# Idle products, an early normalisation and an early copy of the values in a four-layer diffusion backbone

## The chip, the cores and the metric

The kernel runs on 1 core of one Trainium2 chip, in float32. The metric is the device time of one execution in microseconds, lower is better. TensorE (PE in the profile) multiplies matrices, VectorE is DVE, ScalarE is ACT, GpSimd is POOL, and SyncE (SP) issues most transfers.

## The reference

A backbone over 256 noisy latent tokens and 256 context tokens of width 1024, four layers deep. Layer `i` normalises and modulates its input, applies a token mixer of kind `i % 3`, adds the result through a gate, and then applies a gated feed-forward with a width-3 convolution:

```python
for i in range(DEPTH):                       # 4 layers; mixers A, B, C, A
    m_lat = jnp.split((s_lat @ mod_w[i] + mod_b[i])[:, None, :], N_MOD, axis=-1)
    m_ctx = jnp.split(s_ctx @ mod_w[i] + mod_b[i], N_MOD, axis=-1)
    u_lat = _modulate(_rmsnorm(h_lat, g[0]), m_lat[0], m_lat[1])
    ...
    h_lat = h_lat + m_lat[2] * _rmsnorm(o_lat, g[1])
    f_lat = _conv_ffn(_modulate(_rmsnorm(h_lat, g[2]), m_lat[3], m_lat[4]), *ffn)
    h_lat = h_lat + m_lat[5] * _rmsnorm(f_lat, g[3])
```

Mixer A (layers 0 and 3) is full attention with 8 heads of 128, with RMSNorm and rotary embedding on queries and keys. Mixer B (layer 1) is a Hyena long convolution. Mixer C (layer 2) is windowed attention with 16 heads of 64 and a sink logit per head. The softmax of C is `softmax([s0, s_ctx, s_loc])` with the sink's column left out afterwards. The context stream passes through the same layers except for the last.

## The kernel before

Each engine runs its own instruction list, written by hand, and waits on semaphores. Nothing is planned at run time. A weight tile of 1 MB is loaded by SP, split by ACT (`w_hi`) and DVE (`w_lo`) into two rounded parts, and multiplied by TensorE in three products.

**The start.** Layer 0's modulation vectors come from `mod_w[0]`, which is loaded in 24 "units" of 1 MB and 256 columns. `unit_rows(r)` (L616 to L626) multiplies unit `r` with both conditioning vectors: sixteen products into one row block. ACT copies the row (`unit_row`, L1303 to L1308), and `unit_cols` (L628 to L638) turns it into columns with four tiny products. `start_turns(p, v)` (L859 to L873) multiplies the hidden state with a diagonal matrix of inverse norms, which normalises and transposes it. Once the columns of units 0 and 1 are there, DVE makes the first coefficients (`start_mod`), ACT and DVE make the first modulated inputs, and `start_part(0, 0)` (L875 to L890) can begin with the layer's own products. Between these steps stand calls of `idle_products(n)` (L841 to L844). Each makes `n` products of 128x128 whose result nobody reads, and each product has two records in the trace. There are four calls in `before`: 8, 12, 4 and 6 products.

**Layer 0's attention.** Heads and token blocks make pieces `x`. For each, TensorE makes the scores, DVE finds their maximum (`peak`, `negate`), ACT makes exponentials (`exps`), DVE divides by the sum (`normalise`), TensorE transposes (`turn`), ACT copies, and TensorE multiplies with the values (`pv`). On DVE `step(x)` is `normalise(x)` followed by `peak(x + 2)` and `negate(x + 2)`. Before, DVE does `step(-2)`, `step(-1)`, then `finish_mod(0, 1)` and only then `step(0)`. `finish_mod(0, 1)` (L1645 to L1671) waits for the columns of all 24 units and finishes layer 0's gates. On TensorE the last unit's columns stand right after the value tile (`unit_cols()` at L1180), and `turn_gates(0)` stands ahead of the scores of piece 3 (L975). ACT makes the exponentials of piece 1 after it has copied the row of unit 23.

**Layer 2's attention.** Here two heads go together (STEP is 2). Tile 5 of the input projection gives the values. Before, TensorE makes the scores of pieces 0 to 3 after tile 5, then `turn_v` (L953 to L959) transposes the values. ACT does `exps(2, 0)`, `exps(2, 1)`, then `evac(5)`, which copies the value tile out with its bias (L1407), and then the copy of the transposed values (L1428). `turn_v` waits for `evac(5)`.

Of the kernel before, what the change touches and what calls it, by code (L numbers as in the profile page):

```python
# [40 lines left out]
KIND = [i % 3 for i in range(DEPTH)]  # L41
# [129 lines left out]
def build(nc, a, out):  # L171

    es = ExitStack()
    with es:
# [167 lines left out]
        STEP = {i: 1 if KIND[i] == 0 else 2 for i in ATT}  # L342
# [152 lines left out]
        k = MOD0  # L495
# [87 lines left out]
        def _(pe):  # L583
# [44 lines left out]
            def unit_cols():  # L628

                if not turning:  # L630
                    return
                r = turning.pop()
                pe.wait_ge(group_rows, r + 1)
                for cc in range(2):
                    c = 2 * UNIT_COLS[r] + cc
                    last = mm(modp[:, c:c + NMOD * KT + 1:NMOD * KT], MROW[:, r % 2, cc * P:(cc + 1) * P], pick,
                              start=True, stop=True)
                last.then_inc(group_cols, 1)  # L638
# [202 lines left out]
            def idle_products(n):  # L841

                for _ in range(n):
                    mm(bank[3][:, 0:P], ident, PR[:, 0, :], start=True, stop=True)  # L844

            pe.wait_ge(rows_in, 16 * N_ROW_DMAS[0])
            turn_rows(range(EARLY))
            idle_products(8)
            pe.wait_ge(consts_set, 1)
            pe.wait_ge(par_ready, 1)  # L850
            pe.wait_ge(silu_ready, 1)
# [1 line left out]
            def start_unit(r):  # L853

                if r % 2 == 0 and r > 0:
                    pe.wait_ge(mod_final, r // 2)
                unit_rows(r)
# [31 lines left out]
                    last.then_inc(tile_done, 1)  # L889

            start_turns(0, 0)
            idle_products(12)
            start_unit(0)
            unit_cols()
            start_turns(0, 1)
            start_unit(1)
            unit_cols()
            idle_products(4)
            start_unit(2)
            idle_products(6)  # L900
            start_part(0, 0)
            unit_cols()
            pe.wait_ge(rows_late, 16 * N_ROW_DMAS[1])
# [57 lines left out]
            def scores(i, xs):  # L961

                A, G, part = KIND[i] == 0, ahead(NH, i), HEADS[i] // 2
                subs = 1 if HALVES[i][xs[0]][1] < 2 else 2
                for x in xs:
                    h, t = HALVES[i][x]
                    pe.wait_ge(q_roped, roped(i, h))
                    if x >= 4:
                        pe.wait_ge(s_exp, G + x - 3)
                    elif x < 2:  # L970
                        pe.wait_ge(q_roped, turns_ahead(i) + 9 + x)
                    elif x == 2 and A:
                        pe.wait_ge(q_root, norms_ahead(i) + 3)
                    elif x == 3 and i == 0:
                        turn_gates(0)  # L975
                        pe.wait_ge(gr_rows, 1)
                for b in range(subs):
                    for x in xs:
                        h, t = HALVES[i][x]
                        if A:  # L980
                            q, k = QK[:, h, :], QK[:, 8 + h // part, :]
                        else:
                            ps = slice(64 * (h % 2), 64 * (h % 2) + 64)
                            q, k = QK[ps, h // 2, :], KD[ps, h // part, :]
                        if t < 2:
                            ins = mm(s_bank(x), q[:, t * P:(t + 1) * P], k, start=True, stop=True)
                        else:
                            ins = mm(s_bank(x)[:, b * CTX:(b + 1) * CTX], q[:, SEQ + b * P:SEQ + (b + 1) * P],
                                     k[:, SEQ:TOK], start=True, stop=True)
                        if b == subs - 1:  # L990
                            ins.then_inc(s_ready, 1)
# [153 lines left out]
            for i in range(DEPTH):  # L1145
                N = NL[i]
                n0, q0 = FIRST["in", i], PAIR0["in", i]
                if KIND[i] == 1:
                    first_tiles(n0, q0, 2 * i, (TOK, TOK))
                    filter_stage(1)  # L1150
                    for t in range(2, 12):
                        tile(n0 + t, q0 + t, TOK, UH, UL, True, True,
                             after=(lambda k: turn_x1v(2) if k == 5 else None) if t == 11 else None)
                        filter_stage(t)
                        if t in (7, 9):
                            turn_x1v((t - 7) // 2)
                        if t in (8, 10):
                            forward(t // 2 - 4, 0)
                            forward(t // 2 - 4, 1)
                    long_conv()  # L1160
                    arrive = lambda k: pe.wait_ge(c_lo, 8 * (k // 4 + 1))
                    free = lambda b: ((c_fly, 16),)
                else:
                    if i > 0:
                        first_tiles(n0, q0, 2 * i, (N, TOK))
                    issued = 0 if KIND[i] == 2 else 3 if i == 0 else 4

                    def after(k, i=i, t=0, issued=issued):
                        for j in TURN_AT[i].get(t, {}).get(k, []):
                            turn_q(i, j)  # L1170
                        if t == 5 and k == 6:
                            for x in range(issued):
                                scores(i, [x])

                    for t in range(2, 6 if KIND[i] else 5):
                        tile(n0 + t, q0 + t, TOK if t == 5 else N, UH, UL, True, True,
                             after=lambda k, t=t, after=after: after(k, t=t))
                    if KIND[i] == 0:
                        value_tile(n0 + 5, q0 + 5, lambda k, after=after: after(k, t=5))
                    unit_cols()  # L1180
                    while issued < 4 and i > 0:
                        scores(i, range(issued, issued + STEP[i]))
                        issued += STEP[i]
                    for j in range(VCH[i]):
                        turn_v(i, j)
                    attention(i, issued)
                    arrive = lambda k, G=ahead(GROUPS, i): pe.wait_ge(ao_lo, G + k + 1)
                    free = lambda b, i=i: ((p_evac, ahead(NH, i) + NH[i]),) if b < 2 else ((ao_lo, ahead(GROUPS, i) + GROUPS[i] - 3 + b),)

                x_phase(2 * i, UH, UL, arrive, free)  # L1190

                n0, q0 = FIRST["up", i], PAIR0["up", i]
                first_tiles(n0, q0, 2 * i + 1, (N, N))
                for t in range(2, FM):
                    tile(n0 + t, q0 + t, N, UH, UL, True, True)
                x_phase(2 * i + 1, MH, ML, lambda k, b=i * FM: pe.wait_ge(ml_ready, b + k + 1),
                        lambda b, q=q0 + FM: (released(q - 2 + b // 2),))
# [3 lines left out]
        def _(act):  # L1201
# [175 lines left out]
            def attention_in(i):  # L1377
                n0, q0, A = FIRST["in", i], PAIR0["in", i], KIND[i] == 0
# [30 lines left out]
                for t in range(6):  # L1409
                    for k in range(KT):  # L1410
                        for j in TURN_AT[i].get(t, {}).get(k, []):
                            if A and TURNS[i][j] >= 7:
                                q_norm(TURNS[i][j])
                        if n0 + t in UNITS and k % 2 == 1:
                            unit_row(UNITS[n0 + t][k // 2])
                        if t == 5 and k == 5:
                            exps(i, 0)
                    if KIND[i] == 2 and t == 3:
                        bias_hi(i)
                    if t < 5:  # L1420
                        hi(n0 + t + 2)
                    else:
                        exps(i, 1)
                    act.wait_ge(tile_done, n0 + t + 1)
                    evac(t)
                for j in range(VCH[i]):
                    act.wait_ge(v_turned, ahead(VCH, i) + j + 1)
                    f(VT[:, :, j * P:(j + 1) * P], o_bank(i, j).rearrange("p (k d) -> p k d", k=4),  # L1428
                      ACT.Copy).then_inc(v_ready, 1)
# [140 lines left out]
        def _(dve):  # L1570
# [254 lines left out]
            def attention(i):  # L1825
# [62 lines left out]
                    link(ts(q3[0], q3[0], scale, None, ALU.mult))  # L1888
                step(-2)
                step(-1)  # L1890
                if i == 0:
                    finish_mod(0, 1)
                for s in range(NH[i] // W):
                    if s >= KN + 3 and (s - KN - 3) % KN == 0:
                        o_lo((s - KN - 3) // KN)
                    for x in range(W * s, W * s + W):
                        step(x)
                    if s in (4, 5):
                        lo_half(FIRST["out", i] + 1, s - 4)
                for g in range((NH[i] // W - 1 - KN - 3) // KN + 1, GROUPS[i]):  # L1900
# [333 lines left out]
```

## Time and profile before

| | |
|---|---|
| Median of 3 runs | 2180.26 us (2178.58 to 2181.62) |
| The profiled execution | 2182.26 us, of which the span is 2180.5 us |
| Granted TensorE clock, mean over the span | 0.997 |
| PE busy | 2128.0 us, 98% |
| DVE busy | 1448.6 us, 66% |
| ACT busy | 885.2 us, 41% |
| POOL busy | 189.9 us, 9% |

The busy time of an engine is the union of its instructions' spans. The chain that ended last is followed back from the last instruction: at each step to whatever released it. Its shares are PE 86%, DVE 6%, ACT 4%, DMA 2% and issue 1%.

### The profile page before, as it was taken

The numbers are of one execution on the slowest core, as the hardware profiler recorded it, in microseconds if no ns is written. First come the engines' busy times: TensorE is split into PE (matmuls) and PEld (weight loads), VectorE is DVE, ScalarE is ACT, GpSimd is POOL, SyncE is SP. The second block draws the span as 40 slices with busy tenths as digits, with TensorE's granted clock in tenths as the row PEclk, the third lists the DMA queues.
The fourth block names the chain that finished last, engine by engine and source line by source line (L and its number), as shares of the span: only waits on it lengthen the run. The fifth ranks groups of instructions, "written<-read, shape, count | busy, mean of one in ns | idle before, by whom it ended". The sixth has DMA issues, their size and how long they took to land.

```text
span 2180.5 us, 28793 instructions
## 1 busy us (share of the span) xinstructions
PE 2128.0 (98%) x11716; PEld 1749.8 (80%) x11716; DVE 1448.6 (66%) x2200; ACT 885.2 (41%) x1344; POOL 189.9 (9%) x234
## 2 busy tenths in 40 slices
PE   7999999999999999999999998999999999999998
PEld 6777888888787778988888796588888878968996
DVE  3426658878767685578787656855788775656554
ACT  3336443332244433533331245844333223455543
POOL 1000011111010002011110001101111100100110
PEclk9999999999999999999999999999999999999999
DMA  9650335546542212245546531022555553314554
GB/s 317 197 186 12 116 107 164 174 154 206 201 142 96 88 58 78 78 145 164 169 152 220 174 108 59 21 93 91 163 159 169 196 193 122 98 57 147 176 191 145
DMA packets 224404, 304.44 MB, mean 140 GB/s; under 512 B 6860, under 2 KB 152906, under 8 KB 224145
## 3 DMA queue, kind: packets, MB, share of 16 engines
q1 hardware_dynamic: 219904, 289.84, 41.0%
q0 software_dynamic: 3984, 12.60, 1.9%
q8 instruction: 93, 1.52, 0.3%
q14 instruction: 39, 0.31, 0.0%
q10 hardware_dynamic: 384, 0.17, 0.0%
HBM read 301.47 MB, written 1.11 MB: 139 GB/s over the span
## 4 chain that ended last, share of the span: by engine, by line
PE 86%; DVE 6%; ACT 4%; DMA 2%; issue 1%; ACTq 0%; POOL 0%; DVEq 0%
PE lo L658 16%; PE lo L659 16%; PE lo L660 16%; PE lo L758 5%; PE lo L760 5%; PE lo L759 5%; PE hi L758 2%; PE hi L760 2%; PE hi L759 2%; PE lo L1010 2%; ACT w_hi L1210 1%; DMA w_raw<-in_ffn_w_down 1%; DVE w_lo L1586 1%; PE stat L758 1%; PE stat L759 1%
## 5 line engine op out<-in xcount | busy, mean ns | idle before, releaser
L658 PE MATMUL lo<-u_hi,w_hi 128*128 128x512 f32 (+1 forms) x1984 | 703.5, 355 | 3.1 <-DVE conv L2058 1.3
L659 PE MATMUL lo<-u_lo,w_hi 128*128 128x512 f32 (+1 forms) x1984 | 692.2, 349 | 0.0
L660 PE MATMUL lo<-u_hi,w_lo 128*128 128x512 f32 (+1 forms) x1984 | 691.9, 349 | 0.0
L1586 DVE TENSOR_TENSOR w_lo<-w_raw,w_hi 128x2048 fp32r<-128x2048 f32 (+1 forms) x179 | 399.7, 2233 | 336.3 <-ACT w_hi L1210 334.9
L1210 ACT ACTIVATE w_hi<-w_raw 128x2048 fp32r<-128x2048 f32 (+1 forms) x179 | 334.1, 1867 | 487.1 <-DMA w_raw<-in_ffn_w_down 260.9
L658 PEld LDWEIGHTS lo<-u_hi,w_hi 128*128 128x128 f32 x1984 | 376.2, 190 | 63.2 <-issue 14.5
L660 PEld LDWEIGHTS lo<-u_hi,w_lo 128*128 128x128 f32 x1984 | 376.1, 190 | 48.1
L659 PEld LDWEIGHTS lo<-u_lo,w_hi 128*128 128x128 f32 x1984 | 376.2, 190 | 47.2 <-issue 1.0
L1612 DVE SCALAR_TENSOR_TENSOR mod_acc<-mod_raw,silu_c,mod_acc 128x512 f32<-128x512 f32 x504 | 394.4, 848 | 8.9 <-DMA mod_raw<-in_mod_w 8.9
L2167 POOL TENSOR_TENSOR mid_lo<-conv,mid_hi 128x512 fp32r<-128x512 f32 (+1 forms) x88 | 117.5, 1355 | 1051.5 <-ACT mid_hi L1565 1051.5
L758 PE MATMUL lo<-w_hi,mid_hi 128*128 128x512 f32 x374 | 147.6, 395 | 3.2 <-DVE u_raw L1686 2.4
L759 PE MATMUL lo<-w_lo,mid_hi 128*128 128x512 f32 x374 | 145.9, 390 | 0.0
L760 PE MATMUL lo<-w_hi,mid_lo 128*128 128x512 f32 x374 | 145.8, 390 | 0.0
L1554 ACT ACTIVATE conv<-lo,par 128x512 f32<-128x512 f32 (+1 forms) x88 | 58.8, 719 | 145.6 <-PE lo L660 145.6
L1565 ACT ACTIVATE mid_hi<-conv 128x512 fp32r<-128x512 f32 (+1 forms) x88 | 46.6, 577 | 154.3 <-DVE conv L2058 154.3
L2044 DVE SCALAR_TENSOR_TENSOR conv<-lo,par,conv 128x510 f32<-128x510 f32 (+1 forms) x88 | 56.3, 680 | 60.5 <-ACT conv L1554 60.5
L758 PEld LDWEIGHTS lo<-w_hi,mid_hi 128*128 128x128 f32 x374 | 70.2, 188 | 21.2 <-issue 5.4
L760 PEld LDWEIGHTS lo<-w_hi,mid_lo 128*128 128x128 f32 x374 | 70.2, 188 | 15.0
L759 PEld LDWEIGHTS lo<-w_lo,mid_hi 128*128 128x128 f32 x374 | 70.3, 188 | 14.0
L1559 ACT ACTIVATE conv<-conv 128x512 f32<-128x512 f32 (+1 forms) x88 | 50.7, 579 | 71.5 <-DVE conv L2049 70.7
L1010 PEld LDWEIGHTS lo<-ident,probs 128*128 128x128 f32 x352 | 39.3, 143 | 34.0 <-DVE probs L1864 23.0
L1010 PE MATMUL lo<-ident,probs 128*128 128x128 f32 x352 | 56.1, 286 | 10.3 <-DVE probs L1864 9.9
(403 smaller groups left out, 2803.6 us busy)
## 6 DMA issues: line engine op xcount, KB each, us to landing
w_raw<-in_ffn_w_up SPq DMA_DIRECT2D x88, 1024.0 KB, 5.1
mod_raw<-in_mod_w SPq DMA_DIRECT2D x144, 512.0 KB, 4.0
w_raw<-in_ffn_w_down SPq DMA_DIRECT2D x40, 1024.0 KB, 5.1
mod_unit<-in_mod_w SPq DMA_DIRECT2D x24, 1024.0 KB, 6.6
w_raw<-in_a_w_qkv SPq DMA_DIRECT2D x12, 1024.0 KB, 7.2
w_raw<-in_b_w_in SPq DMA_DIRECT2D x12, 1024.0 KB, 5.2
w_raw<-in_a_w_out SPq DMA_DIRECT2D x8, 1024.0 KB, 5.0
w_raw<-in_ffn_w_down SPq DMA_DIRECT2D x8, 512.0 KB, 3.7
```

The costliest lines, as they stand in the source:

```text
L658: mm(o, h3[:, k, c], x, start=(first and k == 0), stop=False)
L659: mm(o, h3[:, k, c], y, start=False, stop=False)
L660: ins = mm(o, l3[:, k, c], x, start=False, stop=(last and k == nr - 1))
L758: mm(o, X[:, kt + j, s], h3[:, j, :], start=first, stop=False)
L759: mm(o, X[:, kt + j, s], l3[:, j, :], start=False, stop=False)
L760: return mm(o, Y[:, kt + j, s], h3[:, j, :], start=False, stop=last)
L1010: last = nc.tensor.transpose(t_bank(i, x)[:, at * P:(at + 1) * P], p[:, src:src + P], ident)
L1210: f(WH[:, n % 3, 0:words], RAW[:, n % 3, 0:words], ACT.Copy).then_inc(hi_ready, 1)
L1554: f(CV[:, m, 0:N], bank[2 * ((q0 + 2 * s) % 2) + m][:, 0:N], ACT.Identity, scale=col("ffn_conv_w", (3 * i + 1) * FM + c), bias=col("ffn_co ...
L1586: tt(WL[:, n % 3, 0:words], RAW[:, n % 3, 0:words], WH[:, n % 3, 0:words].bitcast(F32), ALU.subtract).then_inc(lo_ready, 1)
L1612: stt(acc, MR[:, k % 2, j, :], S2[:, s:s + 1], acc, ALU.mult, ALU.add).then_inc(mod_step, 1)
L2167: tt(ML[:, c, 0:N], CV[:, c % 2, 0:N], MH[:, c, 0:N].bitcast(F32), ALU.subtract).then_inc(ml_ready, 1)
```

## The change

There are three edits.

1. At the start the first call of idle products grows from 8 to 12, the call of 12 ahead of unit 0 goes, and the two calls of 4 and 6 around unit 2 become one of 4 behind it.
2. In layer 0 DVE does `step(0)` ahead of `finish_mod(0, 1)`. TensorE's `unit_cols()` for unit 23 moves behind the first `turn`, into the scores of piece 3 just ahead of `turn_gates(0)`. ACT makes the exponentials of piece 1 ahead of the row of unit 23.
3. In layer 2 the scores of pieces 0 and 1 move into tile 5, behind its step k = 6. ACT copies the value tile and the transposed values ahead of the exponentials of pieces 0 and 1.

```diff
             turn_rows(range(EARLY))
-            idle_products(8)
+            idle_products(12)
...
             start_turns(0, 0)
-            idle_products(12)
             start_unit(0)
             unit_cols()
             start_turns(0, 1)
             start_unit(1)
             unit_cols()
+            start_unit(2)
             idle_products(4)
-            start_unit(2)
-            idle_products(6)
             start_part(0, 0)
...
                     elif x == 3 and i == 0:
+                        unit_cols()
                         turn_gates(0)
...
-                    issued = 0 if KIND[i] == 2 else 3 if i == 0 else 4
+                    issued = 2 if KIND[i] == 2 else 3 if i == 0 else 4
...
                         if t == 5 and k == 6:
-                            for x in range(issued):
-                                scores(i, [x])
+                            for x in range(0, issued, STEP[i]):
+                                scores(i, range(x, x + STEP[i]))
...
-                    unit_cols()
                     while issued < 4 and i > 0:
...
-                        if t == 5 and k == 5:
+                        if t == 5 and k == 5 and A:
                             exps(i, 0)
+                            exps(i, 1)
                     if KIND[i] == 2 and t == 3:
                         bias_hi(i)
                     if t < 5:
                         hi(n0 + t + 2)
-                    else:
-                        exps(i, 1)
                     act.wait_ge(tile_done, n0 + t + 1)
                     evac(t)
+                if not A:
+                    exps(i, 0)
+                    exps(i, 1)
                 for j in range(VCH[i]):
...
                 step(-1)
-                if i == 0:
-                    finish_mod(0, 1)
                 for s in range(NH[i] // W):
...
                     for x in range(W * s, W * s + W):
                         step(x)
+                    if s + i == 0:
+                        finish_mod(0, 1)
```

## Rows read from the trace of the kernel before

**Rows 1.** The page's busy times: engine, us, share, instructions.
```profile
PE 2128.0 (98%) x11716; PEld 1749.8 (80%) x11716; DVE 1448.6 (66%) x2200; ACT 885.2 (41%) x1344; POOL 189.9 (9%) x234
```

**Rows 2.** PE's waits over the span: total us, times, longest us.
```profile
PE lo L1010 <- DVE probs L1864: 9.9, 13, 1.7
...
PE lo L745 <- DVE conv L1706: 2.9, 2, 2.6
...
PE lo L958 <- ACT qkv L1407: 2.1, 1, 2.1
```

**Rows 3.** PE's timeline at the start: start us, us, line, operation, [idle before].
```profile
13.61 2.05 PE L871 MATMUL stat<-conv,h 128*128 128x128 f32 x8 [2.20 <-DVE conv L1706]
15.45 4.61 PE L844 MATMUL lo<-par_rows,ident 128*128 128x128 f32 x24
19.99 1.07 PE L624 MATMUL modp<-mod_unit,silu_c 128*32 128x256 f32 x16
21.56 0.61 PE L636 MATMUL modp<-ident,mod_rows 128*128 128x2 f32 x4 [0.50 <-ACT mod_rows L1308]
22.03 1.14 PE L871 MATMUL hi<-conv,h 128*128 128x128 f32 x8
...
29.58 0.47 PE L885 MATMUL lo<-u_hi,w_hi 128*128 128x512 f32 x1 [0.77 <-DVE u_lo L1643]
```

**Rows 4.** SP's timeline: the issue of unit 0.
```profile
4.63 2.33 SPq L547 DMA_DIRECT2D mod_unit<-in_mod_w  x1
```

**Rows 5.** The DMA view of that transfer: KB, us from issue to landing.
```profile
mod_unit<-in_mod_w SPq DMA_DIRECT2D x1, 1024.0 KB, 12.6
```

**Rows 6.** Idle products, early and late: ns min/median/max, first and last start.
```profile
L844 PE MATMUL lo<-par_rows,ident x16: 420/421/422, 7.8 to 11.0; 128*128 128x128 f32 x16
...
L844 PE MATMUL lo<-par_rows,ident x7: 274/275/312, 19.1 to 19.8; 128*128 128x128 f32 x7
```

**Rows 7.** Two stretches: busy us by engine; the number after POOL is the granted clock.
```profile
155.50:162.00 6.50, 5.07 (x10) 2.42 (x11) 3.82 (x15) 2.99 (x9) 1.66 (x3) 0.51 0.22 83
1978.30:1981.30 3.00, 2.52 (x14) 2.25 (x13) 2.29 (x7) 3.00 (x8) 0.00 (x0) 0.52 0.00 1
```

**Rows 8.** PE's timeline in layer 0's attention.
```profile
156.57 1.11 PE L1010 MATMUL lo<-ident,probs 128*128 128x128 f32 x4 [1.69 <-DVE probs L1864]
...
158.26 2.08 PE L986 MATMUL modp<-qkv 128*128 128x512 f32 x2 [0.36 <-ACT gate_rows L1265]
```

**Rows 9.** ACT's timeline there: the exponentials of piece 0.
```profile
150.31 0.78 ACT L1365 ACTIVATE probs<-hi,small,q_scale 128x512 f32<-128x512 f32 x1 [1.76 <-DVE small L1852]
```

**Rows 10.** DVE's timeline there: the first of `finish_mod`, and `normalise(0)` behind it.
```profile
154.92 0.29 DVE L1659 TENSOR_TENSOR modv<-modp,par 128x32 f32<-128x32 f32 x2 [3.86 <-PE modp L636]
...
156.03 0.49 DVE L1864 TENSOR_SCALAR probs<-probs,small 128x512 f32<-128x512 f32 x1
```

**Rows 11.** PE's timeline in layer 2, from the scores of pieces 0 and 1.
```profile
1333.52 1.13 PE L986 MATMUL hi<-k_dup,qkv 64*128 64x512 f32 x4
...
1337.62 0.66 PE L958 MATMUL lo<-ident,qkv 128*128 128x128 f32 x4 [2.11 <-ACT qkv L1407]
```

**Rows 12.** ACT's timeline in layer 2.
```profile
1331.88 1.28 ACT L1365 ACT_TABLE_LOAD   x1 [3.34 <-POOL probs L2106]
1335.48 0.72 ACT L1365 ACTIVATE probs<-probs,small 128x513 f32<-128x513 f32 x1 [2.32 <-DVE small L1842]
...
1336.90 0.66 ACT L1407 ACTIVATE qkv<-lo,par 128x512 f32<-128x512 f32 x1
1338.31 0.60 ACT L1428 ACTIVATE v_tok<-lo 128x512 f32<-128x512 f32 x1 [0.75 <-PE lo L958]
```

**Rows 13.** DVE's timeline in layer 2: the scaling that ends `normalise(0)`.
```profile
1336.52 0.49 DVE L1864 TENSOR_SCALAR probs<-probs,small 128x512 f32<-128x512 f32 x1
```

**Rows 14.** ACT's timeline at another table load, with no wait behind it.
```profile
572.72 1.28 ACT L1274 ACT_TABLE_LOAD   x1
574.02 0.20 ACT L1274 ACTIVATE inv_o<-eps 128x1 f32<-128x1 f32 x1
```

## The prediction, made before the result was known

> **What bounds the kernel now.** I read the page's busy times first: PE is busy 98% of the span, no other engine over 66% [rows 1]. So the change can only win by taking out PE's idle time, or time in which PE runs slowly. The second view is PE's waits [rows 2]. The reader is to see there that the largest wait is for `normalise` (9.9 us in 13 waits, longest 1.7), and that the wait for layer 2's value copy is one wait of 2.1 us. The third view is the timeline around the three places that the diff touches, and the fourth the lengths and the granted clock there.
>
> These lengths show something that the mean clock of 0.997 hides. The idle products last 421 ns early in the kernel and 275 ns from 19.1 us on [rows 6]. The first is the length at 1.2 GHz, the second at 2.4. The granted clock is 0.51 from 155.5 to 162, in layer 0's attention, and 0.52 at 1978 [rows 7]. Before the first of these PE had waited 0.5 us and then 1.69 us, with only small products between [rows 8]. Before the second it had waited 2.6 us [rows 2]. After the 2.11 us wait of layer 2 the four products of `turn_v` take 0.66 us [rows 11], which is the length at the high clock. So of PE's waits near two microseconds some went with a fall of the clock and one did not.
>
> **Edit 1, the start.** The first call's four more products, at 0.42 us each (two records of 0.21 us spacing), take 1.7 us of the 2.20 us in which PE waits for the first diagonals [rows 3], so they cost nothing. The 12 products after `start_turns(0, 0)` run from 15.45 until the rows of unit 0 at 19.99 [rows 3]. Unit 0 landed at 4.63 + 12.6 = 17.2 us [rows 4, 5]. So its rows can begin at 17.25, which is 2.7 us earlier and no more, since the transfer ends the wait next. With all at the high clock, everything up to `start_part(0, 0)` moves by 2.7 us: the chain from the columns through the coefficients to its first product at 29.58 [rows 3] has no other long wait.
>
> But the clock rose at 19.1, in the midst of those 12 products [rows 6]. Without them PE is idle from about 15.5 to 17.2, after having been idle for the rest of the first gap. I expect the low clock in the following chain. At the low clock `start_turns` takes 2.05 us, not 1.14 [rows 3]: 0.9 more. The rows of a unit (1.07 us, [rows 3]) I double: 0.9 more for each of two. The columns (0.61 us) take some 0.35 more, twice. That is 0.9 + 1.8 + 0.7 = 3.4, and 3.4 - 2.7 = +0.7 us. I take +0.7. The ends: -2.7 if the clock stays high. On the other side the twelve products of `start_part(0, 0)` may still run at the low clock, because four idle products ahead of them cover less than ten did. They stand 0.23 us apart at the high clock and would stand 0.43 apart: 2.4 more, so +3.1. Of what was moved, `start_unit(2)` issues nothing to SP, but the transfers of units 8 to 10 wait for its group and its neighbours. They are not needed for another 20 us.
>
> The Trainium skill's page "TensorE: Matmul & The Clock Gate", section "Part 1: The HAM clock gate (the "warmup" mystery)", says that the half rate is the default and that activity releases it. By that rule idle products are not idle, which speaks against this edit. The trace agrees: 421 ns, then 275 ns, with nothing but such products in between [rows 6]. By the rule the term is +0.7, by the issue order alone it would be -2.7.
>
> **Edit 2, layer 0.** Piece 0's exponentials are finished at 151.2 [rows 9], but DVE's `normalise(0)` stands behind `finish_mod`, which starts at 154.92, so its scaling comes at 156.03 [rows 10] and PE waits 1.69 us [rows 8]. Afterwards `normalise(0)` and `peak(2)` run at 151.2, beside the value tile. The first `turn` (0.5 us at the high clock) goes into the half microsecond in which PE waits for ACT's copy of unit 23's row (the [0.50] of such a copy in rows 3). The columns then end at 154.88 as before (156.57 - 1.69). What is late next is the gates: `finish_mod` still takes until 155.8 [rows 10], and the gates' transposition with ACT's copy takes some 0.7 us. So the scores of piece 3 start at 156.5 in place of 158.26 [rows 8]: 1.7 us earlier. ACT's exponentials of piece 1, moved ahead of the row of unit 23, run at 151.2 to 152.2 where ACT had nothing, and delay no one.
>
> The rest is clock. From 156.57 to 162 all is at half speed [rows 7]: in 158.26 to 161.8 four records of scores take 3.6 us that take 1.8 at the high clock. With the `turn` in the earlier wait, PE's rest is 1.0 and 0.4 us in place of 1.69 and 0.36. If the clock stays up the term is 1.7 + 1.7 = -3.4 (the ACT and DVE steps behind it allow about that). If it falls all the same, -1.7. The rows speak equally for both, so I take the middle, -2.6. The ends are -3.4 and -1.3, the latter if the low stretch lies worse.
>
> **Edit 3, layer 2.** Scores of pieces 0 and 1 take 0.96 us wherever they stand, and the last scores end at 1335.5 (1337.62 - 2.11) as before [rows 11]. Their inputs are there by 1332.2, so the place inside tile 5 does not stall. DVE's first peak then comes 0.7 us earlier. But `exps` now stands behind both copies. The value tile is copied at 1334.75 to 1335.4, hidden by the scores. `turn_v` follows at 1335.5, and the copy of the values at 1336.2 takes 0.60 [rows 12]: 1336.8. Before, ACT's table load (1.28 us) stood right ahead of the first exponentials and ran at 1331.88, while ACT was waiting anyway [rows 12]. It now comes behind the copy: 1336.8 to 1338.1. Where no wait follows such a load, the next activation starts 1.30 us after its start [rows 14]. So the first exponentials start at 1338.1 in place of 1335.48. From there to the end of `normalise(0)` is 1.5 us (1335.48 to 1336.52 + 0.49, [rows 12, 13]). The first `turn` starts at 1339.65, where before it stood behind `turn_v` at 1338.1: 1.5 us late. Piece 1 loses more. DVE does `peak(2)` (0.7 us) between the two normalisations, and before this fitted into the wait for `turn_v`. The second `turn` comes at 1340.95 and the scores of pieces 4 and 5 at 1341.4 in place of 1339.1. In the next pair part of that is caught up, and 2.1 us stay, since this stretch is bound by DVE and ACT and not by PE.
>
> PE's wait grows from 2.11 to 3.55 us (1336.1 to 1339.65). This is longer than the 2.6 us that cost the clock at 1978 [rows 2, 7], so I expect the low clock. It costs up to 2.9 us, the half of layer 0's stretch of 5.7 [rows 7, 8], but here PE has waits of its own that take up a part. I take +1.5, so +3.6 for the edit. The ends are +0.8 (the load hidden after all, and no fall) and +5.0.
>
> The Trainium skill's "ScalarE: Activation LUTs", section "What ACT_TABLE_LOAD costs", gives about 1.28 us for the load and as much again and a little more for a drain, 2.66 in all. The trace agrees with the load and shows no drain (1.30 in all, [rows 14]). By the page's figure the term would be 1.4 us larger, an estimate.
>
> **Sum.** +0.7 - 2.6 + 3.6 = +1.7 us. The profiled execution took 2182.26 (span 2180.5 and 1.8 around it), so 2184.0 by its own time. It lies 2.0 above the median of the runs, so the forecast is 2182.0.
>
> **Rivals.**
> (a) The clock holds at the start and in layer 0, and only layer 2 loses its 2.1: -2.7 - 3.4 + 2.1 = -4.0, 2176.3. For it: 2.1 us of waiting did not lower the clock in layer 2 [rows 11]. Against: PE starts this kernel at the low clock [rows 6].
> (b) The change does what it says in all three places, with the table load hidden: -2.7 - 3.4 + 0.8 = -5.3, 2175.0. Against it is that every load stands right before its user.
> (c) Slower: the clock. PE is starved at the start and in layer 2, the low clock lasts into `start_part(0, 0)` and into the attention's first pairs: +3.1 - 1.3 + 5.0 = +6.8, 2187.1. It decides if the clock is still low when `start_part(0, 0)` begins near 30 us, and falls again near 1338. For it: [rows 7]. Against: PE recovered within 6.5 us in layer 0.
> (d) The waits are hidden by later ones anyway and nothing changes: 2180.3. Against it is that PE has hardly any idle time that could take them up.
>
> **Chances.** Forecast 0.50, (a) 0.17, (b) 0.10, (c) 0.18, (d) 0.05. No change can be told from within 0.2%, about 4.4 us. Faster than 2175.9 are most of (b) and half of (a): 0.15. Slower than 2184.6 are (c) and a tenth of the forecast's own spread: 0.22. The rest is 0.63. The range is 2176.0 to 2186.5.
>
> **What would show each step.** Rows of unit 0 at 17.25 and 1.9 us long, not 1.07; the first product of `start_part(0, 0)` at 30, not at 26.9. In layer 0 a `turn` before the columns of unit 23, and the scores of piece 3 at 1.7 us less than the shift of the start. In layer 2 a table load between the copy of the values and the first exponentials, and a wait of PE of over 3 us ahead of the first `turn`. The prediction is wrong if the start gains 2.7, if the load is not there, or if the clock stays at 1.00 in both attentions.

## The result, and the profile after

| | before | after |
|---|---|---|
| Median, 7 runs each on one chip | 2181.62 us (2178.58 to 2183.85) | 2187.82 us (2185.05 to 2189.93) |
| Span of the profiled execution | 2180.5 us | 2187.1 us |
| Granted clock, mean | 0.997 | 0.994 |

The change makes the kernel slower: the ratio of the times is 1.0032, with a 95% interval of 1.0023 to 1.0042, so 6 to 7 us (5 to 9 by the interval). The forecast was 2182.0, its range ended at 2186.5, and "slower" had a chance of 0.22. The prediction was wrong.

The page's busy times hardly move, as in [rows 1]. Only the count tells something: 28 products and 28 weight loads fewer.

```profile
PE 2128.7 (97%) x11688; PEld 1745.7 (80%) x11688; DVE 1449.4 (66%) x2200; ACT 885.5 (40%) x1344; POOL 191.0 (9%) x234
```

**The start.** PE's timeline of after, as [rows 3]: start, length, line, operation, [idle before].

```profile
8.31 4.15 PE L844 MATMUL lo<-par_rows,ident 128*128 128x128 f32 x24
14.13 1.13 PE L871 MATMUL stat<-conv,h 128*128 128x128 f32 x8 [1.67 <-DVE conv L1706]
17.74 1.86 PE L624 MATMUL modp<-mod_unit,silu_c 128*32 128x256 f32 x16 [2.48 <-DMA mod_unit<-in_mod_w]
20.96 2.05 PE L871 MATMUL hi<-conv,h 128*128 128x128 f32 x8
30.28 0.47 PE L885 MATMUL lo<-u_hi,w_hi 128*128 128x512 f32 x1 [1.56 <-DVE u_lo L1643]
...
45.92 0.63 PE L887 MATMUL lo<-u_hi,w_lo 128*128 128x512 f32 x1
46.35 0.63 PE L885 MATMUL lo<-u_hi,w_hi 128*128 128x512 f32 x1
```

The rows of unit 0 start 2.25 us earlier and take 1.86 us in place of 1.07. The first product of `start_part(0, 0)` comes 0.70 us later. Then, at 45 us, the products stand 0.43 us apart, which is the low clock. Before, they stood 0.23 apart there.

**Stretches and their clock.** The view of stretches of after (length, busy time of PE, PEld, DVE, ACT, POOL, granted clock, DMA share, GB/s), as [rows 7]:

```profile
17.90:24.60 6.70, 6.22 (x44) 3.67 (x36) 2.29 (x1) 0.49 (x2) 0.00 (x0) 0.50 1.10 348
24.70:45.10 20.40, 16.14 (x141) 11.86 (x137) 9.11 (x26) 7.36 (x14) 0.00 (x0) 1.00 1.10 350
45.20:48.50 3.30, 3.30 (x9) 2.52 (x10) 0.40 (x5) 0.00 (x0) 0.00 (x0) 0.50 1.11 350
155.50:162.00 6.50, 5.17 (x34) 3.12 (x27) 3.39 (x16) 4.24 (x12) 1.18 (x3) 1.00 0.50 164
1338.90:1352.40 13.50, 11.85 (x38) 6.07 (x40) 7.71 (x29) 9.12 (x23) 1.55 (x6) 0.50 0.01 3
```

Two low stretches are new at the start, that of layer 0 is gone, and layer 2 has one of 13.5 us.

**Layer 0.** PE's timeline of after around the gates, as [rows 8]:

```profile
156.02 0.66 PE L1009 MATMUL lo<-ident,probs 128*128 128x128 f32 x4
156.68 0.58 PE L636 MATMUL modp<-ident,mod_rows 128*128 128x2 f32 x4
158.22 0.28 PE L611 MATMUL modp<-ident,gate 128*32 128x128 f32 x1 [0.97 <-DVE gate L1669]
158.86 1.13 PE L985 MATMUL modp<-qkv 128*128 128x512 f32 x2 [0.35 <-ACT gate_rows L1263]
```

**Layer 2.** First PE's, then ACT's timeline of after, as [rows 11] and [rows 12]:

```profile
1335.59 0.66 PE L956 MATMUL lo<-ident,qkv 128*128 128x128 f32 x4
1338.23 0.66 PE L1009 MATMUL lo<-ident,probs 128*128 128x128 f32 x4 [1.98 <-DVE probs L1864]
1339.49 1.11 PE L1009 MATMUL lo<-ident,probs 128*128 128x128 f32 x4 [0.61 <-DVE probs L1864]
1340.54 2.08 PE L987 MATMUL hi<-k_dup,qkv 64*128 64x256 f32 x8
```

```profile
1334.64 0.69 ACT L1405 ACTIVATE qkv<-lo,par 128x512 f32<-128x512 f32 x1 [6.36 <-PE lo L660]
1335.35 1.28 ACT L1363 ACT_TABLE_LOAD   x1
1336.64 0.72 ACT L1363 ACTIVATE probs<-probs,small 128x513 f32<-128x513 f32 x1
1337.36 0.71 ACT L1363 ACTIVATE probs<-probs,small 128x513 f32<-128x513 f32 x1
1338.07 0.57 ACT L1428 ACTIVATE v_tok<-lo 128x512 f32<-128x512 f32 x1
```

The value tile's copy comes first, then the table load, then both exponentials, and the copy of the transposed values last. `turn_v` has no wait now, and the wait stands one step later, ahead of `turn(0)`.

**The end.** PE's last wait of after for split weights, and beside it the DMA view of the stretch in which that weight tile comes (2161.7 to 2168.5: GB/s in 40 slices, PE's instruction queue, and the transfer with its KB and its time from issue to landing):

```profile
2172.73 0.50 PE L758 MATMUL stat<-w_hi,mid_hi 128*128 128x512 f32 x1 [2.82 <-DVE w_lo L1586]
```

```profile
GB/s 0 96 0 0 0 0 72 133 12 60 24 157 313 386 398 386 386 386 373 446 398 386 398 361 398 362 109 12 12 24 24 24 24 24 24 24 36 0 0 0
...
q8 instruction: 1, 0.02, 1.0%
w_raw<-in_ffn_w_down SPq DMA_DIRECT2D x1, 1024.0 KB, 6.6
```

Before, the tile of the same number landed in 5.0 us and PE waited 1.22. Nothing of the change stands in this part of the code. The difference of the traces, point by point, counted at the issues of weight tiles, is this (after less before, us):

| | first product | 66 us | 235 us | 1315 us | 1465 us | last tile, 2157 us | end |
|---|---|---|---|---|---|---|---|
| after | +0.70 | +2.30 | -0.73 | -0.26 | +5.39 | +5.03 | +6.65 |

So the start loses (1.6 between the first product and 66 us), layer 0 gains 3.0, layer 2 loses 5.65, and the last tile's wait loses 1.6 more. One trace can't say what of this is the change and what is chance. In the seven kernels of this document that keep the start of before (two of them with a filler in PE's first wait), the first product comes anywhere from 28.15 to 29.58 us, since the first transfers land at other times and the clock rises at other times (the first record of a high clock starts at 19.1 us in before, at 10.6 in `layer0_only` below). The trace of before is the latest of the seven, and its execution took 2 us more than the median. So each edit was run alone.

### The profile page after: what moved, and what is told of

Same layout as the page of the kernel before. It is cut to its first block, busy times and chain, and to the rows that moved or that the text cites. A ratio compares the mean times of both kernels' runs of the same rounds, so it can differ in the third digit from the quotient of the medians.

```text
span 2187.1 us, 28737 instructions
## 1 busy us (share of the span) xinstructions
PE 2128.7 (97%) x11688; PEld 1745.7 (80%) x11688; DVE 1449.4 (66%) x2200; ACT 885.5 (40%) x1344; POOL 191.0 (9%) x234
## 3 DMA queue, kind: packets, MB, share of 16 engines
q8 instruction: 93, 1.52, 0.3%
## 4 chain that ended last, share of the span: by engine, by line
PE 85%; DVE 7%; ACT 4%; DMA 3%; issue 1%; SPq 0%; POOL 0%; ACTq 0%; DVEq 0%; POOLq 0%
PE lo L658 16%; PE lo L659 15%; PE lo L660 15%; PE lo L758 5%; PE lo L760 5%; PE lo L759 5%; PE hi L758 2%; PE hi L760 2%; PE hi L759 2%; ACT w_hi L1208 2%; PE lo L1009 2%; DMA w_raw<-in_ffn_w_down 1%; DVE w_lo L1586 1%; PE stat L758 1%; PE modp L624 1%
## 5 line engine op out<-in xcount | busy, mean ns | idle before, releaser
L2058 DVE TENSOR_TENSOR conv<-conv,lo 128x512 f32<-128x512 f32 (+1 forms) x88 | 50.5, 616 | 29.4 <-PE lo L660 29.4
```

## Experiments

All ratios are against the kernel before on the same chip, with 11 runs of each kernel and 15 to 33 of before. "At 66", "at 235" and so on are shifts of the profiled execution against before, as in the table above.

**Each edit alone.** `start_only` has edit 1's lines of the diff and nothing else. `layer0_only` has `unit_cols()` behind `turn(0)`, the exponentials of piece 1 ahead of unit 23's row (for layer 0) and `finish_mod(0, 1)` behind `step(0)`. `layer2_only` has `issued = 2` with pairs of scores in tile 5 and both exponentials behind the value tile's copy.

> The kernel before with edit 1 alone. Clock theory: the idle products taken out let the clock fall before unit 0, and what the earlier unit gains is paid back by the slow chain, so +0.2 to +2.5 us against the kernel before, with the first product of start_part(0, 0) within 0.5 us of where it was. Rival (the edit is free or a gain, and layer 2 alone makes the loss): -1 to 0 us, with the clock high from unit 0 on. Rival (the start is half of the loss): +3 us.

> The kernel before with edit 2 alone. Both theories: a gain. Reordering with the clock held: -3.2 us (what the two traces show). If the clock falls all the same in this attention: -1.7 us. If the gain in the trace of after came from the start's shift: 0 us.

> The kernel before with edit 3 alone. Theory: this edit makes the whole loss, +5.6 us, with a table load between the value tile's copy and the first exponentials and a granted clock of 0.50 for some 10 us behind it. Rival (the clock's fall there was chance of one execution): +1.5 to +2.5 us.

| | median, before's | ratio (95%) | at 66 | 235 | 1315 | 1465 | 2157 | end |
|---|---|---|---|---|---|---|---|---|
| start_only | 2186.20, 2180.42 | 1.0026 (1.0017 to 1.0035) | +1.98 | +1.93 | +1.91 | +1.88 | +3.88 | +6.70 |
| layer0_only | 2178.18, 2180.42 | 0.9994 (0.9985 to 1.0003) | -1.41 | -4.57 | -4.28 | -4.32 | -2.80 | -2.60 |
| layer2_only | 2182.14, 2180.42 | 1.0008 (1.0000 to 1.0017) | -1.10 | -0.81 | -0.45 | +2.17 | -0.21 | -0.26 |

The medians give +5.8, -2.2 and +1.7, in all +5.3 of the 6.2. Two of the expectations missed. `start_only` was given +3 at most, and no theory had a far part. `layer2_only` was to make the whole loss, and only the time of its rival, +1.5 to +2.5, was met. `layer0_only` lies between its -3.2 and -1.7. Its trace gains 3.2 in layer 0 and loses 1.8 near 1881 us, in layer 3, where the clock fell for 3.3 us. The same fall came in `best_mid` and `after_filled`, behind a wait of 1.43 us that every kernel has there, before too. Whether it is chance stays open.

Edit 1 is nearly the whole loss, and two thirds of it aren't at the start: its trace is at +1.9 from 66 us to the last layer, and then goes to +6.7. These are PE's two waits in which that happens, and the DMA view of the stretch around the transfer that the first one waits for (2106.3 to 2114.1, first the share in tenths), all in `start_only`:

```profile
2117.96 0.50 PE L758 MATMUL lo<-w_hi,mid_hi 128*128 128x512 f32 x1 [3.11 <-DVE w_lo L1584]
...
2171.18 0.71 PE L758 MATMUL stat<-w_hi,mid_hi 128*128 128x512 f32 x1 [2.42 <-DVE w_lo L1584]
```

```profile
DMA  0002021607899899999999511000000000098017
GB/s 0 0 0 84 0 32 63 137 11 168 263 357 389 305 441 357 431 357 431 378 378 378 200 32 11 11 21 32 21 32 21 32 21 21 32 126 84 21 53 231
...
q8 instruction: 1, 0.02, 0.7%
```

The second wait cost more than its own length, for the clock fell behind it. The view of stretches of `start_only`:

```profile
2171.30:2174.70 3.40, 3.40 (x9) 2.63 (x10) 0.00 (x0) 0.00 (x0) 0.00 (x0) 0.50 0.00 0
```

Eight products stand 0.43 us apart there in place of 0.23, 1.6 of the 2.8 us between 2157 us and the end.

In the DMA view the reader is to see the tail. The 16 DMA engines move some 380 GB/s together, so 24 is one of them. Most of the 1 MB is there after 4.5 us, and then one engine works alone for another 2 us. A packet of the queue "q8 instruction" falls into this stretch. By its count that queue carries PE's instructions: the page lists 93 packets and 1.52 MB of it for 23,376 products and weight loads, so 16 KB and some 250 instructions to a packet.

This made a theory. The edit takes 56 instructions out of PE's list, so each later packet is asked for at another point of the work. In the last layer a weight tile is issued about every 5.8 us and lands in 5.0, and where a packet meets one, this one can land 1 to 3 us late, and PE waits. The Trainium skill's "Runtime: NRT & Kernel Launch", section "Instruction fetch mechanics", says that every engine fetches its instructions in blocks of 16 KiB, 256 instructions each, over a DMA queue of its own. The packets here agree in size and number. The same page of the Trainium skill calls the fetch mostly hidden. PE shows no wait for instructions here, but a weight transfer beside it isn't spared.

**The count of instructions.** `start_padded` is edit 1 with 14 tiny products (56 instructions of PE, like those taken out, see below) in PE's first wait. `before_pad10` is the kernel before with ten of them. `after_padded` is after with 14. `start_late` is edit 1 with the 14 in the wait ahead of `turn_v` in layer 2.

```diff
+            for _ in range(14):
+                mm(bank[3][0:32, 0:2], ident[:, 0:32], pick, start=True, stop=True)
             pe.wait_ge(rows_in, 16 * N_ROW_DMAS[0])
```

> Edit 1 alone, and 14 tiny products (128x32 weights, two columns, 56 instructions on PE with their weight loads) in PE's first wait, where it waits for the parameter rows: as many instructions as edit 1 takes out. Fetch theory: edit 1 costs some 4 us at the far end of the kernel, because 56 instructions fewer move all of PE's instruction transfers (16 KB each) against the weight transfers of the last layer, and those that start together land late. Then the padding brings the landings of the last layer back to those of the kernel before, and the time to +1 to +2.5 us. Clock theory (all of edit 1's cost is the start's own): +5 to +6 us, as without the padding.

> The kernel before, all its idle products kept, and 10 such tiny products (40 instructions) in PE's first wait. Fetch theory: the transfers of PE's instructions move by 40 places, and from the trace of before some six of them (it was three or four) would then start within 1.5 us of a weight transfer of the last layer, so +1.5 to +5 us with late landings at other tiles than before. Clock theory: the early wait is not on the path, so 0 us.

> The changed kernel with 14 tiny products in PE's first wait. Fetch theory: 4 us of its 6.2 us loss go away, so +1 to +3 us against the kernel before. Clock theory: +5 to +7 us, no change.

> Edit 1 alone, with the 14 tiny products not in PE's first wait but in the 2.1 us wait of layer 2 ahead of turn_v, some 1330 us later. Theory (the 56 instructions that edit 1 took out move the instruction packets against the last layer's weight transfers): the start is that of edit 1 alone, +1.9 us up to layer 2, the wait of layer 2 hides most of the products, and the weights of the last layer land in about 5 us again: the median is 1 to 3 us above before, like the kernel with the products at the start (+1.65), and not 5.8 above. Rival (it is the start itself, or the engine awake in its first wait, that decides): the last layer's late landings stay and the median is 5 to 7 us above before.

Late landings are those over 6.1 us among the last 31 of the 182 weight tiles in the profiled execution, read transfer by transfer (the nearest below that line are one of 6.06 in `start_padded` and one of 6.00 in `start_late`):

| | median, before's | ratio (95%) | at 66 | 1465 | 2157 | end | late |
|---|---|---|---|---|---|---|---|
| before | | | | | | | 1 |
| start_only | 2186.20, 2180.42 | 1.0026 (1.0017 to 1.0035) | +1.98 | +1.88 | +3.88 | +6.70 | 5 |
| start_padded | 2181.68, 2180.03 | 1.0009 (1.0000 to 1.0018) | +2.72 | +2.67 | +0.42 | +0.29 | 0 |
| start_late | 2181.90, 2179.75 | 1.0008 (0.9999 to 1.0017) | +2.65 | +2.86 | +0.62 | +0.55 | 0 |
| before_pad10 | 2182.51, 2180.03 | 1.0013 (1.0005 to 1.0022) | -0.40 | +0.15 | +0.80 | +0.72 | 4 |
| after | 2187.82, 2181.62 | 1.0032 (1.0023 to 1.0042) | +2.30 | +5.39 | +5.03 | +6.65 | 4 |
| after_padded | 2182.30, 2180.03 | 1.0013 (1.0004 to 1.0022) | -0.11 | +2.56 | -0.35 | -0.37 | 0 |

The trace of before pays for its own late landing (7.8 us, issued at 2021.5), so between 1465 and 2157 us kernels without one gain some 2 us on it that their medians don't show.

The theory holds. The 14 products make edit 1 4.1 us faster though the start isn't faster at all (+2.7 at 66 us). They do so too when they stand 1330 us later, where the start is edit 1's own, so it isn't PE being awake in its first wait. The same filler put into before, where it only shifts the count, costs 2.5 us in the median (its trace, with four late landings, shows 0.7 of it). In after it brings back about 4. Of the 7.0 us between the two traces 2.4 are the start, where `after_padded` has no second low stretch, and 4.2 stand behind 1465 us. Here are the same two waits in `start_late`, and its DMA view for the same tile (2104.9 to 2110.7): no packet, no tail.

```profile
2114.24 0.50 PE L758 MATMUL lo<-w_hi,mid_hi 128*128 128x512 f32 x1 [0.77 <-DVE w_lo L1587]
...
2166.66 0.50 PE L758 MATMUL stat<-w_hi,mid_hi 128*128 128x512 f32 x1 [1.16 <-DVE w_lo L1587]
```

```profile
GB/s 0 0 0 0 0 0 0 71 127 85 28 0 42 141 395 410 410 410 410 395 395 438 395 410 395 410 438 410 410 367 226 14 0 0 0 0 0 0 0 0
...
w_raw<-in_ffn_w_down SPq DMA_DIRECT2D x1, 1024.0 KB, 4.9
```

The 14 traces of this document together tie the late landings to the packets. The last 31 weight transfers of each are 434, and 20 of them are late. In 62 a packet of PE's queue starts in the first 4 us behind the issue, and 19 of the late ones are among these. Of the other 372 one is late. The ten kernels with as many PE instructions as before have 0 to 2 late landings, the two with 56 fewer 5 and 4, those with 8 and 40 more 3 and 4.

Not every meeting costs: in `start_only` a packet came within 0.2 us of the issue at 2028.7, and that tile landed in 4.9 us. In the ten kernels with the count of before a packet starts 0.2 to 0.9 us behind the issue of the same tile, the 25th from the end, which lands in 5.2 to 7.8 us. The view doesn't tell on which of the 16 engines a packet lay, so what makes the difference stays open. A product leaves two records for the matrix product and two for the weight load, hence 56 for 14.

**The table load of layer 2.** `layer2_preload` is `layer2_only` with one tiny exponential on ACT ahead of its wait for tile 5, so that the table is loaded while ACT waits anyway.

```diff
+                    if t == 5 and not A:
+                        f(R1[:, 1, 4:5], eps[:, :], ACT.Exp)
                     act.wait_ge(tile_done, n0 + t + 1)
```

> Edit 3 alone, with one tiny exponential on ACT ahead of the wait for tile 5, so that the table load runs while ACT waits. Theory (the exposed load starts it, the clock multiplies it): the exponentials start 1.3 us earlier, PE's wait shrinks below 1 us, the clock stays up, and the time is that of the kernel before or less, -1 to +0.5 us. Rival (the order behind the copy costs by itself): +3 us or more with the load hidden.

Median 2180.17 against 2180.42, ratio 0.9998 (0.9989 to 1.0007). From 1315 to 1465 us it changes by -0.2, where `layer2_only` loses 2.6. ACT's, then PE's timeline:

```profile
1328.17 1.28 ACT L1425 ACT_TABLE_LOAD   x1
...
1335.10 0.71 ACT L1365 ACTIVATE probs<-probs,small 128x513 f32<-128x513 f32 x1
```

```profile
1336.67 0.66 PE L1010 MATMUL lo<-ident,probs 128*128 128x128 f32 x4 [0.56 <-DVE probs L1869]
1337.94 0.66 PE L1010 MATMUL lo<-ident,probs 128*128 128x128 f32 x4 [0.61 <-DVE probs L1869]
```

Theory and time came as expected. The load is the cause of the long wait (1.98 us in `layer2_only` as in after, 0.56 here), and the copy ahead of the exponentials brings nothing even without it.

**The clock of layer 2.** `after_filled` is after with 6 tiny products at the start and 8 idle products of 128 columns right behind `turn_v` of layer 2, 56 instructions in all.

```diff
+                    if i == 2:
+                        for _ in range(8):
+                            mm(bank[3][:, 0:P], ident, ident, start=True, stop=True)
                     attention(i, issued)
```

> The kernel after, with 6 tiny products in PE's first wait and 8 idle products of 128 columns just ahead of layer 2's attention: 56 PE instructions in all, as many as edit 1 took out, so that the last layer meets its instruction packets as before does. Theory (the wait ahead of turn(0) of layer 2 lets the clock fall, and that fall is most of edit 3's loss there): the granted clock stays at 1.00 through layer 2's attention, the stage loses about 1.3 us against before (the bare table load) rather than 5.6, and the median comes to 2178 to 2180 us, 2 to 4 under the after with 14 tiny products (2182.3). Rival (the loss in layer 2 is the wait itself and not the clock): the stage still loses 4 to 6 us and the median stays at 2182 to 2183.

Median 2180.50 against 2180.47, ratio 1.0000 (0.9991 to 1.0008). PE's timeline, and the stretch with its clock:

```profile
1332.76 0.66 PE L958 MATMUL lo<-ident,qkv 128*128 128x128 f32 x4
1333.26 1.95 PE L1188 MATMUL lo<-ident 128*128 128x128 f32 x16
1335.40 0.66 PE L1011 MATMUL lo<-ident,probs 128*128 128x128 f32 x4 [0.20 <-DVE probs L1869]
```

```profile
1331.00:1352.00 21.00, 18.21 (x117) 10.78 (x118) 16.40 (x57) 18.96 (x47) 2.89 (x10) 1.00 0.15 51
```

The exponentials come when they came, yet the stage loses 1.26 us (from -3.09 to -1.83) and not 5.65. So of edit 3's 5.65 us in after's trace 1.3 are the load and 4.4 the low clock. The median is 0.5 above the range of the theory.

**The parts that pay.** `l0_scores` has the start of before, edit 2, and of edit 3 only the earlier scores, with ACT's order as before. `best_mid` is the same with 12 and 8 in the first two idle calls of the start, not 8 and 12. `best_pad2` is `l0_scores` with two tiny products more in PE's first wait.

> The start of the kernel before, edit 2, and of edit 3 only the earlier scores of layer 2; its exponentials stay ahead of the value tile's copy. Theory: -3.2 us from layer 0 where the clock held, of which the median may show less, and -0.9 us in layer 2 (the first peak and exponentials 0.9 us earlier): -2.5 to -4.1 us in all. Rival (the scores inside tile 5 are themselves the cost in layer 2): 0 us or slower, with a wait inside tile 5.

> The start of before, edit 2, and of edit 3 only the earlier scores, with 12 idle products in the first of the two idle groups of the start and 8 in the second, rather than 8 and 12; the number of instructions is unchanged. Theory: PE's order is what binds between 19.99 and 22.03 us, so the clock holds as before and nothing after unit 0 moves by more than 0.5 us: the median stays within 1 us of the 2176.1 of the kernel with 8 and 12. Rival: the first group's four more products push unit 0's turns past the clock's rise and the clock falls early, as with edit 1: 1.5 to 2 us more.

> The same kernel (start of before, edit 2, earlier scores) with 2 tiny products, 8... rather 2 products and 2 weight loads' worth of instructions, more in PE's first wait. Theory (the place of PE's instruction packets against the weight transfers of the last layer sets some of its time): the first products of the last layer move by so few instructions that at most one late landing comes or goes: within 1.5 us of 2176.1, to either side. Rival (the number of instructions does not matter): within 0.3 us, and the landings of the last layer's weights stay as they were.

| | median, before's | ratio (95%) | late |
|---|---|---|---|
| l0_scores | 2176.10, 2180.03 | 0.9982 (0.9973 to 0.9991) | 0 |
| best_mid | 2176.41, 2180.47 | 0.9981 (0.9972 to 0.9990) | 0 |
| best_pad2 | 2177.38, 2180.47 | 0.9984 (0.9975 to 0.9993) | 3 |

`l0_scores` is 4 us faster than before, as expected, and `best_mid` is as fast within the intervals. The `turn_v` of `l0_scores` waits half as long as in [rows 11]:

```profile
1332.55 0.66 PE L958 MATMUL lo<-ident,qkv 128*128 128x128 f32 x4 [1.02 <-ACT qkv L1407]
```

`best_mid` tells what edit 1 could have been worth. The rows of unit 0 begin as soon as it lands and the clock stays up until layer 0, the best that edit 1 can do. PE's timeline of `best_mid`, then of `l0_scores`:

```profile
17.17 1.07 PE L624 MATMUL modp<-mod_unit,silu_c 128*32 128x256 f32 x16 [0.87 <-DMA mod_unit<-in_mod_w]
26.76 0.47 PE L885 MATMUL lo<-u_hi,w_hi 128*128 128x512 f32 x1 [0.76 <-DVE u_lo L1645]
31.74 0.50 PE L885 MATMUL lo<-u_hi,w_hi 128*128 128x512 f32 x1 [0.96 <-DVE w_lo L1588]
37.89 1.07 PE L624 MATMUL modp<-mod_unit,silu_c 128*32 128x256 f32 x16 [0.66 <-DVE coef L1626]
```

```profile
28.15 0.47 PE L885 MATMUL lo<-u_hi,w_hi 128*128 128x512 f32 x1 [0.77 <-DVE u_lo L1645]
37.84 1.07 PE L624 MATMUL modp<-mod_unit,silu_c 128*32 128x256 f32 x16 [0.66 <-DVE coef L1626]
```

The first product comes 1.39 us earlier (0.5 was expected at most), and 11 us later nothing of that is left, since the next weight tile isn't split yet. `best_pad2` has three late landings, where one at most was expected to come or go, and 1.3 us more in the median, with intervals that overlap. Two of the three are at tiles that land late in kernels with the count of before too, so it doesn't settle anything.

## Why the prediction was wrong

**Edit 1, the near part: right in kind, short in size.** The low clock came as predicted, the rows took 1.86 us and the first product came 0.70 us late (+0.7 predicted). That this number fits is partly luck, since the trace of before starts late: on average the first product comes 1.0 us later in the six kernels with edit 1's start than in the seven with the start of before. The working stopped at `start_part(0, 0)`. It took the later products as either all slow or all fast, and in after the second low stretch (45.2 to 48.5) cost 1.6 us more. It came in four of the six. Those four stand at +2.0 to +2.7 at 66 us, the other two, `after_padded` and `after_filled`, at -0.1 and -0.3, and the seven with the start of before at -1.45 to 0. So the near part is some 2.4 us on average, inside the ends of -2.7 to +3.1. The end of -2.7 was wrong: the working said that the chain to the first product has no other long wait, but behind that product `best_mid` shows a wait for weights that takes the gain back. So rivals (a) and (b) held a gain that didn't exist. And one reading was wrong. Between the idle products of 421 ns and those of 275 stand not only such products but also the first `start_turns` and PE's wait of 2.20 us ahead of it [rows 3].

**Edit 1, the far part: the step that failed.** The silent premise was that what is removed costs or saves only where it stood. The edit 1 term has no line for the 56 instructions that leave PE's list, so it put their effect at nothing without a reason. The change measured +6.2 us where the sum had +1.7, and these instructions are the larger part of the difference. They cost about 4 of edit 1's 5.8 us, some 2100 us later, as the two kernels with the filler show (2181.68 and 2181.90 in place of 2186.20). With that part taken out, the whole change is worth +2.3 in the median (`after_padded`), next to the sum of +1.7. That the two are so near is in part luck: in the trace of `after_padded` layer 0 gives -3.2 (-2.6 predicted), layer 2 +5.7 (+3.6) and the start -0.1 (+0.7).

**Edit 2: right.** -2.6 was a middle between a clock that stays (-3.4) and one that falls (-1.7). It fell in all seven kernels without edit 2, stayed in six of the seven with it, and fell in `best_mid`, for 3.4 us in place of 6.8. The stage gained 2.9 to 3.2 in the six (3.0 in after, 3.2 alone) and 1.9 in `best_mid`, so the edit mostly keeps the clock up too, where the prediction gave both cases the same weight. The median of `layer0_only` gives -2.2, which its interval doesn't tell from none. `turn(0)` before the columns and the shorter waits of 0.97 and 0.35 us came as told.

**Edit 3: right in kind, wrong in its order and its size.** I put the exponentials behind both copies, and so does the section on the change. In the diff they stand between them, ahead of the loop that copies the transposed values, so that the first starts at 1336.64 and not after the transposed values' copy. PE's waits are 1.98 and 0.61, not one of 3.55. The load lies open as predicted and costs 1.3. The clock fell as predicted, but after a wait shorter than the one that I gave as its reason, and for 13.5 us: 4.4 us where I had +1.5. The 5.65 us lie beyond the end of +5.0 that I gave, and this excess of 2 us over +3.6 is the second part of what the sum lacked in after's trace. Alone the edit had a low stretch of 3.3 us (1339.0 to 1342.3, clock 0.50) and cost 2.6 in the trace, 1.7 in the median. So +3.6 was too little in after's trace and too much for the edit alone, and the size of this term depends on how long the clock stays down.

Rival (c), with 2187.1, came nearest to the time, but not by its mechanism. Of the two signs that it named one came: the clock fell again near 1338 us (+5.65, +5.0 in the rival), but it was high when `start_part(0, 0)` began. The start lost 2.3 us where the rival had 3.1, and 1.6 of them in the stretch behind 45 us. Its layer 0 fall didn't come, and it had no far part either.

## What to carry to other kernels

An edit that changes the number of an engine's instructions moves every later fetch of its code, and where 1 MB transfers pace the end of a kernel this alone was worth 4 us here. So compare two versions at an equal count of instructions, with fillers in a wait, before you judge what an edit does. Idle products hold the clock for the work behind them: take them out only where the next real wait is short, and put some where a new wait appears. An activation table is best loaded by a dummy operation in a wait of ACT.

## What the runs showed of the hardware

- In the last layer a weight tile of 1 MB lands in 5.0 us. The late ones took 6.2 to 7.8 us, 19 of the 20 with a packet of PE's instructions in the first 4 us, and in the two shown above one DMA engine was left to finish alone at about 24 GB/s.
- In layer 2 the clock fell behind a wait of PE of 1.98 us, and not behind one of 2.11 us [rows 11] or waits of 0.56 and 0.61. The low stretch of the same code lasted 3.3 us in `layer2_only` and 13.5 in after.
- The exponential starts 1.29 us after the start of the 1.28 us table load (1335.35 to 1336.64). The Trainium skill's "ScalarE: Activation LUTs", section "What ACT_TABLE_LOAD costs", gives 2.66 us with a drain. No drain is seen here, as in [rows 14].
